# Splitting the remaining fp32 products in two rounded parts, with filler products in TensorE's waits, in a kernel of four layers on one Trainium2 core

## The reference

```python
proj = x @ w_in + b_in          # pool, q, k, v, index q, index k, index w, memory q, gates
branches = (pool_branch(...),   # windowed means, a 128x128 mix per group, times pool_scale
            dsa_branch(...),    # index scores pick 64 keys a query, then softmax attention
            memory_branch(...)) # mem @ w_mem_kv gives keys and values, softmax attention
for n in range(3):
    merged = merged + sigmoid(gates[n]) * (branches[n] @ w_br[n])
x = layer_norm(DN_ALPHA * x + merged @ w_out, ln1_g, ln1_b)
x = layer_norm(DN_ALPHA * x + moe(x), ln2_g, ln2_b)     # 16 experts, the best 2 of one group
```

```python
z = rms(x) @ w_in_2             # sliding-window heads, forgetting heads, mLSTM heads
y = concat(swa_attention, fox_attention, sigmoid(o) * rms(mlstm))
x = x + y @ w_out_2
x = x + square(relu(rms(x) @ w_ff1)) @ w_ff2
```

## Time and profile before

| | us |
|---|---|
| median of 3 runs (1936.44 to 1942.44) | 1938.91 |
| the profiled execution | 1939.55 |
| its span in the trace | 1938.1 |
| TensorE, matmuls busy | 1696.5 |
| TensorE, weight loads busy | 1260.8 |
| VectorE busy | 779.3 |
| ScalarE busy | 669.4 |
| mean granted clock of TensorE | 0.92 |

### The profile page before, as it was taken

The page is one execution under the profiler, slowest core; times in us unless marked ns, Lnnn a source line. Parts: engine busy times, 40 slices in busy tenths (PEclk is TensorE's granted clock), DMA queues, the critical chain, the costliest instruction groups (busy, mean ns, idle before and its releaser), DMA issues.

```text
span 1938.1 us, 22103 instructions
## 1 busy us (share of the span) xinstructions
PE 1696.5 (88%) x9198; PEld 1260.8 (65%) x9198; DVE 779.3 (40%) x1480; ACT 669.4 (35%) x1077; POOL 29.5 (2%) x49
## 2 busy tenths in 40 slices
PE   6998997999887998996999877858999987689998
PEld 5777995433336777995433327744899886448997
DVE  5455345111116355345101016552555463525554
ACT  4336432111114236432111114442444345325442
POOL 4000000000000000000000000000000000000000
PEclk9999998899998998998999998867999998579999
DMA  9432446799994431445899983400455443004553
GB/s 290 174 109 87 153 152 239 295 421 421 421 400 152 167 116 72 155 172 217 344 421 421 421 364 115 171 1 22 142 184 196 152 156 150 0 22 153 184 185 109
DMA packets 57807, 393.72 MB, mean 203 GB/s; under 512 B 7140, under 2 KB 7184, under 8 KB 15712
## 3 DMA queue, kind: packets, MB, share of 16 engines
q1 hardware_dynamic: 54288, 381.35, 51.0%
q0 software_dynamic: 3264, 9.61, 1.8%
q10 hardware_dynamic: 144, 1.24, 0.2%
HBM read 391.11 MB, written 1.05 MB: 202 GB/s over the span
## 4 chain that ended last, share of the span: by engine, by line
PE 75%; DVE 10%; DMA 9%; ACT 4%; issue 1%; SPq 0%; POOL 0%; DVEq 0%; ACTq 0%; POOLq 0%
PE psum L549 72%; DMA ring_sb<-in_weights 8%; PE psum L677 2%; PE psum L594 1%; DMA router_w_sb<-in_w_router 1%; ACT ring_rounded L1145 1%; DVE xT_lo_rounded L1899 1%; ACT region_sb L1171 1%; DVE ring_rounded L1511 1%; DVE x_sb L1624 1%; DVE x_sb L1622 0%; DVE region_sb L1916 0%; DVE region_sb L1919 0%; DVE small_sb L1912 0%; DVE region_sb L1910 0%
## 5 line engine op out<-in xcount | busy, mean ns | idle before, releaser
L549 PE MATMUL psum<-ring_sb,region_sb 128*64 128x512 f32 (+1 forms) x1728 | 433.6, 602 | 39.4 <-DMA ring_sb<-in_weights 26.0
L1511 DVE TENSOR_TENSOR ring_rounded<-ring_sb,ring_rounded 128x2048 fp32r<-128x2048 f32 (+4 forms) x152 | 321.6, 2130 | 227.0 <-ACT ring_rounded L1145 226.9
L549 PE MATMUL psum<-xT_hi_rounded,ring_rounded 128*128 128x256 f32 x1920 | 353.6, 286 | 0.0
L549 PEld LDWEIGHTS psum<-ring_sb,region_sb 128*64 128x64 f32 (+1 forms) x1728 | 151.4, 144 | 300.1 <-issue 282.0
L1145 ACT ACTIVATE ring_rounded<-ring_sb 128x2048 fp32r<-128x2048 f32 (+4 forms) x152 | 268.9, 1781 | 177.2 <-PE psum L549 144.5
L549 PEld LDWEIGHTS psum<-xT_hi_rounded,ring_rounded 128*128 128x128 f32 x1920 | 304.4, 195 | 1.9 <-issue 0.5
L549 PE MATMUL psum<-xT_lo_rounded,ring_rounded 128*128 128x256 f32 x960 | 283.8, 296 | 5.8 <-DVE xT_lo_rounded L1899 5.8
L549 PE MATMUL psum<-ring_rounded,xT_hi_rounded 128*128 128x384 f32 (+4 forms) x832 | 234.3, 358 | 21.2 <-DVE ring_rounded L1511 15.1
L549 PE MATMUL psum<-ring_rounded,region_rounded 128*128 128x512 f32 x960 | 223.7, 393 | 3.0 <-DVE region_rounded L2119 3.0
L549 PEld LDWEIGHTS psum<-ring_rounded,region_rounded 128*128 128x128 f32 x960 | 180.4, 189 | 41.2 <-DVE region_rounded L2119 3.4
L549 PEld LDWEIGHTS psum<-xT_lo_rounded,ring_rounded 128*128 128x128 f32 x960 | 187.4, 195 | 8.7 <-DVE xT_lo_rounded L1899 6.2
(11 more groups left out here) (247 smaller groups left out, 1353.7 us busy)
## 6 DMA issues: line engine op xcount, KB each, us to landing
ring_sb<-in_weights SPq DMA_DIRECT2D x324, 1024.0 KB, 8.5
ring_sb<-in_weights SPq DMA_DIRECT2D x24, 768.0 KB, 4.3
ring_sb<-in_weights SPq DMA_DIRECT2D x8, 904.0 KB, 4.6
ring_sb<-in_weights SPq DMA_DIRECT2D x8, 900.0 KB, 4.6
ring_sb<-in_weights SPq DMA_DIRECT2D x8, 584.0 KB, 10.7
region_sb<-in_mem POOLq DMA_DIRECT2D x2, 1024.0 KB, 8.4
region_sb<-in_pool_band POOLq DMA_DIRECT2D x2, 1024.0 KB, 9.6
region_sb<-in_ln_g POOLq DMA_DIRECT2D x4, 512.0 KB, 4.3
```

The lines of the kernel that those rows point to most:

```text
L549: return nc.tensor.matmul(dst, lhsT, rhs, start=first, stop=last, skip_group_check=True)
L1511: nc.vector.tensor_tensor(rounded(piece.raw), piece.raw, reread(piece.hi), ALU.subtract).then_inc(lo_made, 1)
```

## The change

It does these things:

- `w_mem_kv`, `w_br` and `w_out_2` pieces are split, 28 in all, and the other operands too. The memory is turned on the host and loaded turned; ScalarE rounds it (`mem_hi`), VectorE writes its rest. Branch outputs and `yT` are written rounded by ScalarE; VectorE then reads the same psum tile and writes the rest: `lower_pool`, `lower_mem`, `lower_dsa`, `lower_values`. The loose bank is freed by VectorE's step instead of ScalarE's.
- The plan is reordered: memory queries before memory keys and values, and each half's projection between its two gate pieces. The calls of `round_hi` and `round_lo` move accordingly. In the first block VectorE rotates q and k before `top(1, ...)`, and shares out memory probabilities one merge step earlier.
- `pe_busy(n)` issues n fp32 products of the identity with 256 columns of a constant into the next free bank. Nobody reads them. There are 307 in the program, at 21 places.

```diff
+        def pe_busy(products, banks=None):
+
+            i, free = (banks or loose).next_free()
+            pe.wait_ge(*free)
+            for _ in range(products):
+                matmul(psum[:, i, 0:S], ident, upto[:, 0, :], True, True)
...
             if l:
+                pe_busy(11)
                 pe_turn_x(l, 0, [x_normed.at(l - 1, 2 + b) for b in range(TB)])
...
             pe_turn(("iq", l), turned, 512, [iqT_made.at(l, n) for n in range(2)], iq_roped.last(l))
-            pe_turn(("memT", l), mem_rows, D, [memT_made.at(l, n) for n in range(4)], landed(mem_in, l, 1))
             pe_turn(("ik", l), turned, P, [ikT_made.at(l)], ik_roped.last(l))
...
             pe_index(l, 1, range(0, 4))
+            query_piece(0)
+            pe_index(l, 1, range(4, 8))
+            query_piece(1)
             key_piece(0)
-            pe_index(l, 1, range(4, 8))
+            pe_busy(4)
+            pe_turn(("q", l), turned, 512, [qT_made.at(l, n) for n in range(2)], q_roped.at(l, 1))
             key_piece(1)
-            pe_rows(("mv", l), [memT], BRANCH, [mv_made.at(l, b) for b in range(TB)], memT_made.last(l))
-            query_piece(0)
-            query_piece(1)
-            pe_turn(("q", l), turned, 512, [qT_made.at(l, n) for n in range(2)], q_roped.at(l, 1))
             pe_turn(("k", l), turned, 512, [qT_made.at(l, 2 + n) for n in range(2)], q_roped.at(l, 3))
+            pe_rows(("mv", l), [mem_hi, memT], BRANCH, [mv_made.at(l, b) for b in range(TB)], mem_split.at(l, 1))
...
+            pe_busy(3)
             pe_held(l, "mixed", [merged_upper, mergedT], [merged_lo.at(l, c) for c in range(4)])
 
         def tensor_route(l):
             E = N_EXPERTS
+            pe_busy(12)
             pe_turn_x(l, 1, [x_normed.at(l, b) for b in range(TB)])
+            pe_busy(2)
...
+            pe_busy(10)
             i, free, full = loose.take(("order", l), slots_made.at(l, 0))
...
+            if l == 0:
+                pe_busy(18)
             pe_turn_rms(l, 0, [ff_added.last(l - 1)] if l else [x_normed.at(first_layers - 1, 3)])
+            pe_busy(3)
...
             pe_swa_values(l, 0)
+            pe_busy(7, dense)
             pe_mls_gates(l, 0)
+            pe_busy(28, dense)
             pe_turn(("fox_q", l), fox["turned"], 256, [fox_qk_made.at(l, 0)], fox_normed.last(l))
...
             pe_swa_values(l, 1)
+            pe_busy(11, dense)
             pe_turn_probs(("mls_probs", l, 0), mls["probs"], MLSTM_HEADS, 1, [mls_turned.at(l, 0)], mls_scored.at(l, 3))
...
-            pe_held(l, "attended", [yT], [mls_y.at(l)] * 4)
+            pe_held(l, "attended", [yT, y_lower], [y_lo.at(l, MLS_LO)] * 4)
```

More of the change, by code:

```diff
@@ L162, in of, with next_free @@
         return self.place[key]
+    def next_free(self):
+        i = (self.turn + 1) % self.count
+        return self.first + i, self.freed.get(i, (self.full[i], 0))
 class Piece:
@@ L1298, in scalar_mix @@
             cut(6)
+            a.wait_ge(*landed(mem_in, l, 1))
+            nc.scalar.activation(rounded(mem_hi), memT, ACT.Copy).then_inc(mem_split.sem, 1)
             index(1, range(0, 4))
+            query_piece(0)
+            index(1, range(4, 8))
+            round_hi(first + 18)
+            query_piece(1)
             key_piece(0)
-            index(1, range(4, 8))
+            round_hi(first + 19)
+            for n in range(2):
+                act_turned(("q", l), n, 2, qT[:, 2 * n:2 * n + 2, :], qT_made)
             key_piece(1)
-            round_hi(first + 20 + 2)
+            round_hi(first + 20)
+            for n in range(2):
+                act_turned(("k", l), n, 2, kT[:, 2 * n:2 * n + 2, :], qT_made)
+            round_hi(first + 22)
             for b in range(TB):
@@ L1465, in scalar_second @@
             act_sink(l, 1)
-            act_values(("swa_out", l, 0), 4, lambda pair: yT[:, pair, 0:P], swa_out)
+            act_values(("swa_out", l, 0), 4, lambda pair: rounded(yT[:, pair, 0:P]), swa_out)
+            round_hi(first + 16)
             act_mls_weights(l, 0)
@@ L1757, in vector_mix @@
             pool_in(range(2, 4))
+            lower_pool(range(2, 4))
             round_lo(first + 2 * 6 + 5)
             index(1, range(0, 4))
+            v.wait_ge(*mem_split.at(l, 0))
+            nc.vector.tensor_tensor(rounded(memT), memT, reread(mem_hi), ALU.subtract).then_inc(mem_split.sem, 1)
             index(1, range(4, 8))
-            round_lo(first + 20 + 2)
-            top(1, range(0, 8))
+            round_lo(first + 18)
             v.wait_ge(*z_made.at(l, 13))
@@ L1768, in vector_mix @@
             rope_heads(C_K, 1)
+            round_lo(first + 20)
+            top(1, range(0, 4))
+            round_lo(first + 22)
+            top(1, range(4, 8))
             mem_scores(0)
@@ L1786, in vector_mix @@
             dsa_shares(1)
-            for dc in range(8):
+            merge(1, 0)
+            merge(1, 1)
+            lower_dsa(1)
+            for dc in range(2, 8):
                 merge(1, dc)
@@ L1965, in swa_shares, with lower_values @@
                 vec_shares("swa", b, swa["probs"], SWA_HEADS, (b + 1) * P, swa_shared)
+            def lower_values(name, out_made, b, pairs, row):
+                for pair in range(pairs):
+                    i, _ = loose.of((name, l, b, pair))
+                    v.wait_ge(*out_made.at(l, pairs * b + pair))
+                    nc.vector.tensor_tensor(rounded(y_lower[:, row + pair, b * P:(b + 1) * P]), psum[:, i, 0:P],
+                                            reread(yT[:, row + pair, b * P:(b + 1) * P]), ALU.subtract).then_inc(y_lo.sem, 1)
             def decays():
```

164 lines of the change are left out of this document (105 added, 59 removed).

## The result

The changed kernel takes 1921.6 us (median of 8 runs, 1914.6 to 1929.7) beside 1939.1 for the kernel before on the same chips. The ratio is 0.9914, with a 95% interval from 0.9896 to 0.9931. It is faster by more than the uncertainty, as forecast, but by 17 us and not by 65: 1921.6 lies outside the range of 1840 to 1910.

A forecast was written before the change was run, and what follows sets the result against it. TensorE's work, waits and clock were taken as the bound. First blocks with the start 35 us less, second blocks 29, together 65 off the median 1938.9, so 1874; range 1840 to 1910.

The forecast's parts named there:

- Keys, values, queries: First block, a layer: split keys 2.7 us less, split values 2.9 less, wait for rotated queries gone, net 4.6 less.
- The load rule: Rival, under 1%: weight loads run in series with products, the 352 split products lose some 60 us; near 1970.
- First branch: First block's first branch projection, interleaved with attention: put at 0, between 7 us less and 4 more.
- Index key's turn: First block: turn starts after some 2.3 us idle without the memory's turns, so 1.7 us added (0 to 2).
- Route: First block, normalised x to experts: fillers before waits shrink slow work; 5 us on the path, net 3.7 less.
- Starts of the second block: 18 fillers (8.2 us) in a wait of 16.6 at the second block's start: 2.5 us less.
- Heads of the second block: Sliding heads' turns 1.3 us less by fillers; ScalarE's roundings add 1.0 and 1.8, VectorE's lowering before the gates 1.1.
- the tail's fillers: Second block's tail: 5.1 us less from full clock; slow turns and products shortly before 2.2, last turns and values 2.5 less.
- the eleven: Eleven fillers (5.0 us) before the second block's first mLSTM turn meet no wait: 3 us more, between 0 and 5.
- The second rule: Second block's tail: TensorE busy without a gap, yet clock stays 1.2 GHz; twice 5.1 can be lost, sum then 1884.
- fillers overrun: Rival, 4%: fillers delay awaited results on in-order TensorE, 2026, slower than before; decides from 0.2 us overrun per filler.
- only the splits and the order pay: Rival, 15%: the clock still falls, since fillers end before their waits do; 28 us less: 1912.

The follow-up runs named there:

- Without the 23: Changed kernel without the 11, 8, 2 and 2 fillers between the sliding heads' values and the last values of each second block: 1905.7 us, 0.9825.
- five for thirteen: Changed kernel without those 11, 8, 2 and 2 fillers, and five instead of thirteen ahead of the last turn of the forgetting probabilities: 1901.4 us, 0.9792.
- later roundings: Changed kernel with the four roundings of the second block's output weights moved out of the heads' stretch, into their engines' waits: 1907.1 us, 0.9845.
- the moved code: Changed kernel with fulfilled waits added to VectorE's program, 225 and 287 instructions more ahead of the two late-token branches: 1916.5 us, 0.9867.

## Why the prediction was wrong

- **Keys, values, queries** held: 18.6 of 20.4. **Other branches** held to 0.1. The load rule, as a rival, is out: 12 rounded products take 1.58 us, where the estimate in that rival, 0.64 for three, makes 2.6.
- **First branch**, put at 0 with a range up to 4 more a layer, cost 0.1 and 3.4. The mark that I named, a stretch above 53 us, wasn't reached over the stretch of the earlier trace rows (49.4 and 50.3).
- **Index key's turn**: 1.7 a layer within 0 to 2; 2.6 (outside) and 1.4 measured. The mechanism was right, an idle of 2.17 us and slow products behind it.
- **Route** 4.5 and 3.5 for 5.0; the **start of the second layer** gave none of its 2. **Starts of the second block**: 2.5 was booked for each layer, though the 18 fillers that it rests on stand only ahead of the first; 0.5 and 2.7 were measured there.
- **Heads of the second block**: the two roundings of ScalarE and the lowering were put at 3.9 a layer and the stretch came within 1.4 of the sum. That is two errors that cancel, and luck. With the roundings and lowerings taken out the stretch is 5.6 and 6.8 shorter, not 3.9, and 3.9 and 6.1 below the kernel before, where I had booked 1.3 for the fillers' clock. The experiments show 14 us to be had there by another order. What failed was also a step not taken: having priced a delay on the path, I did not ask whether the saving (5.5) was worth it, or where else the rounding fits.
- **Output projection** held: 7.7 a layer for 7.4.
- **The failed step is the tail's fillers.** It said: "They stand before waits and delay nothing while they are shorter", with the eleven as the one exception in the tail, at 3 us. In the tail that was never checked group by group. The eight meet no wait, which the row of the kernel before shows (values 0.91 us behind the turn, no idle time). In the two layers they cost 3.9 and 4.1. The eleven took 5.3 in the first of the two layers, and the stretch around them grew by 6.9, since the values ahead of them ran at low clock and lost 1.7. In the second layer the kernel before had that low clock too, and the stretch grew by 3.5. The four around the scores cost 3.9 and gave 2.9, where I had booked 5.1 for the clock alone. The thirteen overran in one layer, where the first of them fell on half clock, by 2.5. Without the 23, and with five for thirteen, 16 and 20 us come back: this step is shown by the runs.
- **The second rule** was stated rightly and booked wrongly. The row showed TensorE busy without a gap at 1.2 GHz, so that these narrow products did not raise the clock. I let it threaten one term of 5.1, while it bears on every group in the tail: behind each, narrow products follow, and the clock falls again among them.
- **Not foreseen at all**: the 5 us behind the first branch of the late tokens, from VectorE's longer code. The trace of before had the same stall at its second branch, 4.95 us on "issue", unexplained; it was there to be asked about.
- **The rivals**: fillers overrun, which I gave 4% as a case by itself, is what happened in the tail. It has no threshold over all 307, as I wrote; it is one group at a time. Removing or shortening some of them gave 16 to 20 us, and the same device, well placed, is worth 25. With that, later roundings and the moved code, 1870.7 was reached. That this lies near the forecast of 1874 is chance: the sum had neither the later roundings nor the moved code. Nearest in time to the changed kernel came *only the splits and the order pay*, 1912, but not by its mechanism: the clock did rise, and splits and order alone gave half of its 28.

## What to carry over

Before filling a wait, find for each filler the idle time *behind* it in the trace, on its own side of the turn, and take its length at half clock: a filler costs its full duration where none stands. Low clock is worth time only where TensorE's own work sets the end; here the low clock fell by 165 us, and the fillers that did it gave 3. When code is added, look at the first instruction behind each taken branch: a stall of 5 us can come and go with the number of instructions ahead of it.

## What the runs showed of the hardware

- A jump of 216 instructions over skipped code left VectorE idle for 0.2 to 0.4 us or for 4.2 to 5.6, by its place in the code (seven places); TensorE showed 3.6 to 4.5 us at the same points in each kernel with fillers there.
- 56 filler records of 128 rows in a row kept the clock at full (14.0 us, 0.25 each). Among products of 64 and 8 rows without a gap it fell: in the changed kernel at 1269.4 among the first forgetting scores (0.48 a pair of records, then 0.79) and again at about 1303.5, in both cases with TensorE busy throughout.
- Executions of one kernel differ by 10 us and more (1871.5 to 1887.9 in one case); in the two that were compared, the difference lay where the clock falls.
